# Hybrid decoder trunk: the remaining input projections are put between the attention steps

## The reference

```python
for l in range(DEPTH):                     # DEPTH = 2, SEQ = 512, D_MODEL = 1024
    h = rmsnorm(x, norm_mix_pre[l])
    z = h @ w_in[l]
    z_sc, z_cf, z_moba, z_mla = jnp.split(z, SPLITS, axis=-1)
    y_a = short_conv_mixer(z_sc, conv_a[l])                    # B * causal_dwconv3(C * h')
    y_b = conformer_conv_mixer(z_cf, conv_b[l], ...)           # GLU, depthwise conv of 31 taps, LayerNorm, swish
    y_c = moba_attention(z_moba, cos_c, sin_c)                 # 4 heads of 64
    y_d = mla_attention(z_mla, g_q, g_kv, w_uq, w_ukv, ...)    # latents 384 and 128, 4 heads of 96
    y = jnp.concatenate([y_a, y_b, y_c, y_d], axis=-1) @ w_out[l]
    x = x + rmsnorm(y, norm_mix_post[l])
    f = conv_ffn_block(rmsnorm(x, norm_ffn_pre[l]), w_ffn_up[l], conv_ffn[l], w_ffn_down[l])
    x = x + rmsnorm(f, norm_ffn_post[l])
```

## Time and profile before

| what | value |
|---|---|
| median of 3 runs | 1291.59 us |
| the runs | 1283.93, 1291.59, 1292.61 us |
| profiled execution, whole | 1292.75 us |
| its span (first to last instruction) | 1291.0 us |
| mean granted TensorE clock | 0.967 |
| PE, PEld, DVE, ACT, POOL busy | 95%, 80%, 66%, 46%, 18% |

### The profile page before, as it was taken

One profiled execution on the slowest core, in us unless ns is written; L12 is line 12 of the kernel. 1 busy time (PEld: TensorE's weight loads), 2 busy tenths in 40 slices (PEclk: granted clock), 3 DMA queues, 4 the chain that ended last, 5 costly groups with the idle time before them and its releaser, 6 DMA issues.

```text
span 1291.0 us, 15584 instructions
## 1 busy us (share of the span) xinstructions
PE 1227.7 (95%) x6036; PEld 1032.0 (80%) x6036; DVE 847.3 (66%) x1178; ACT 591.7 (46%) x889; POOL 233.3 (18%) x208
## 2 busy tenths in 40 slices
PE   5997999999999999999999799999899999999997
PEld 5885878888888888888898587788788888888885
DVE  4699576587666666544669977565686666665453
ACT  3453367454444444434545534664454444444432
POOL 1284167020000000000006733551100000000000
PEclk8998988999999999999999999599999999999998
DMA  7222202352333333456632230025333333335563
GB/s 235 78 67 82 76 1 82 115 162 84 98 98 95 94 94 97 156 190 210 196 96 78 63 92 33 1 86 173 101 114 98 98 98 96 95 96 185 181 215 128
DMA packets 155676, 143.17 MB, mean 111 GB/s; under 512 B 6447, under 2 KB 137427, under 8 KB 155603
## 3 DMA queue, kind: packets, MB, share of 16 engines
q1 hardware_dynamic: 154480, 140.40, 35.7%
q10 hardware_dynamic: 1123, 1.79, 0.4%
HBM read 140.07 MB, written 2.10 MB: 110 GB/s over the span
## 4 chain that ended last, share of the span: by engine, by line
PE 80%; DVE 12%; POOL 3%; issue 2%; DMA 2%; ACT 1%; SPq 0%; POOLq 0%; DVEq 0%; ACTq 0%
PE ps L459 26%; PE ps L460 25%; PE ps L461 25%; DVE cf_out L1040 4%; DVE wsp L391 2%; PE ps L670 2%; POOL prob L805 1%; POOL rms_r L763 1%; DMA x<-in_x 1%; DVE rot L937 1%; DVE xn L881 1%; DMA raw<-in_w_ffn_up 1%; DVE shuf L935 1%; DVE hid L942 1%; PE ps L514 1%
## 5 line engine op out<-in xcount | busy, mean ns | idle before, releaser
L459 PE MATMUL ps<-xn,wsp 128*128 128x512 f32 (+2 forms) x1136 | 421.6, 371 | 20.8 <-DVE xn L881 15.9
L460 PE MATMUL ps<-xn,wsp 128*128 128x512 f32 (+2 forms) x1136 | 418.4, 368 | 0.0
L461 PE MATMUL ps<-xn,wsp 128*128 128x512 f32 (+2 forms) x1136 | 418.2, 368 | 0.0
L391 DVE TENSOR_TENSOR wsp<-raw,wsp 128x1024 fp32r<-128x1024 f32 (+2 forms) x250 | 306.6, 1228 | 160.5 <-ACT wsp L383 160.3
L383 ACT ACTIVATE wsp<-raw 128x1024 fp32r<-128x1024 f32 (+1 forms) x256 | 266.9, 1043 | 186.3 <-PE ps L461 152.2
L459 PEld LDWEIGHTS ps<-xn,wsp 128*128 128x128 f32 (+1 forms) x1136 | 217.0, 191 | 59.1 <-DVE xn L881 18.1
L461 PEld LDWEIGHTS ps<-xn,wsp 128*128 128x128 f32 (+1 forms) x1136 | 216.6, 191 | 35.5
L460 PEld LDWEIGHTS ps<-xn,wsp 128*128 128x128 f32 (+1 forms) x1136 | 216.9, 191 | 35.0 <-issue 0.5
L459 PE MATMUL ps<-wsp,hid 128*128 128x512 f32 (+1 forms) x488 | 189.7, 389 | 0.0
L461 PE MATMUL ps<-wsp,hid 128*128 128x512 f32 (+1 forms) x488 | 189.1, 388 | 0.0
L460 PE MATMUL ps<-wsp,hid 128*128 128x512 f32 (+1 forms) x488 | 189.1, 387 | 0.0
(11 more groups left out here) (136 smaller groups left out, 1367.6 us busy)
## 6 DMA issues: line engine op xcount, KB each, us to landing
raw<-in_w_ffn_up SPq DMA_DIRECT2D x88, 512.0 KB, 3.8
raw<-in_w_ffn_down SPq DMA_DIRECT2D x88, 512.0 KB, 3.9
raw<-in_w_in SPq DMA_DIRECT2D x40, 512.0 KB, 3.8
raw<-in_w_out SPq DMA_DIRECT2D x32, 512.0 KB, 3.5
x<-in_x SPq DMA_DIRECT2D x4, 512.0 KB, 9.6
out_x<-x SPq DMA_DIRECT2D x4, 512.0 KB, 3.9
raw<-in_w_uq SPq DMA_DIRECT2D x4, 288.0 KB, 2.9
gain_mix<-in_norm_mix_post SPq DMA_DIRECT2D x2, 512.0 KB, 4.8
```

Of the source, the lines that this page charges most:

```text
L391: eng.tensor_tensor(wsp[:, u % SPLIT, 1, 0:nk * n], raw[:, (l * NU + u) % RAW, 0:nk * n], fp(wsp[:, u % SPLIT, 0, 0:nk * n]), ALU.subtract ...
L459: pe.matmul(dst, a[0], b[0], start=start, stop=False, skip_group_check=True)
L460: pe.matmul(dst, a[0], b[1], start=False, stop=False, skip_group_check=True)
L461: return pe.matmul(dst, a[1], b[0], start=False, stop=stop, skip_group_check=True)
```

## The change

Groups 10 and up lose their place ahead of attention. After group 10 (`ckv`) the attention loop begins at once, and the other projections, the MLA products, the three `stat` and `spread` pairs and the mean of the LayerNorm are issued by `fill(p)` at the head of the steps `p` that the table `AT` names. They share two PSUM banks, 4 and 7, in turn, and each waits until the one before the last has been taken out of its bank (`weave_free`). The loop has 34 places: two without scores lie between the MoBA and the MLA heads. The splits of the weights are put at the steps of `SPLIT_AT`. W_out's order of rows becomes `OUT_ORDER`, and seven rows of its first half are issued in the last eight places of the loop. Of the conformer's second half DVE does the first 7 taps, ACT and POOL the other 24 (6 ahead of the loop, 18 in it, one a step); of the first half 10 taps lie ahead of the loop and 21 in it. MLA queries, keys and values get tiles in `hid` in place of `xn`, since `xn` is still read. The scaled rows and the exponentials share one buffer of four (`sp`), where `sm` had two and `prob` three.

```diff
+OUT_ORDER = (4, 5, 0, 1, 6, 2, 3, 7)
+
+
+G_CF, G_QK, G_V, G_CKV = 0, 4, 8, 10
+GROUP = dict(ckv=10, cq0=11, cq1=12, cq2=13, sc0=14, kr=15, mq0=16, mq1=17, mk0=18, mk1=19, sc1=20, mq2=21, mq3=22,
+             mk2=23, sc2=24, mv0=25, mv1=26, mk3=27, sc3=28, sc4=29, sc5=30)
+G_UP = 31
 NG = G_UP + 2 * NF
...
+SCORE0, PT_BANKS, PV_BANKS = 5, (2, 3), (0, 1)
 RING = (0, 1, 2, 3, 5, 6, 7)
-PV_BANKS = (0, 1, 7)
+WEAVE_BANKS = (4, 7)
+WEAVE = ("ckv", "cq0", "stat_ckv", "cq1", "spread_ckv", "cq2", "stat_cq", "sc0", "spread_cq", "kr", "mq0", "mq1", "mk0",
+         "mk1", "sc1", "mq2", "mq3", "mk2", "sc2", "mv0", "mv1", "mk3", "mean", "sc3", "sc4", "stat_ln", "sc5",
+         "spread_ln")
+
+AT = dict(cq0=1, stat_ckv=2, cq1=3, spread_ckv=4, cq2=5, stat_cq=8, sc0=8, spread_cq=10, kr=11, mq0=14, mq1=14, mk0=15,
+          mk1=15, sc1=16, mq2=17, mq3=17, mk2=18, sc2=19, mv0=20, mv1=20, mk3=21, mean=23, sc3=24, sc4=26, stat_ln=27,
+          sc5=29, spread_ln=30)
 UP_BANKS = (4, 5, 6, 7)
...
-CF_VECTOR = {3: 2, 4: 1, 5: 1, 6: 1, 7: 1, 8: 4, 9: 4, 10: 4, 11: 2, 12: 4, 13: 4, 14: 3}
-CF_SCALAR = {3: 1, **{g: 3 for g in range(4, 14)}}
-assert sum(CF_VECTOR.values()) == CF_TAPS and sum(CF_SCALAR.values()) == CF_TAPS
+
+
+CF_LEAD = 7
+CF_SECOND = {3: 2, 4: 1, 5: 1, 6: 1, 7: 1, 8: 1}
+CF_FIRST = {8: 2, 9: 3, 10: 5}
+CF_SCALAR = {8: 2, 9: 2, 10: 2}
+CF_FIRST_STEP = {**{p: 1 for p in range(18)}, 2: 2, 6: 2, 10: 2}
+CF_SCALAR_STEP = {p: 1 for p in range(18)}
+assert sum(CF_SECOND.values()) == CF_LEAD
+assert sum(CF_FIRST.values()) + sum(CF_FIRST_STEP.values()) == CF_TAPS
+assert sum(CF_SCALAR.values()) + sum(CF_SCALAR_STEP.values()) == CF_TAPS - CF_LEAD
 N_ATT = 2 * HEADS * TC
-NPROB = 3
+NPROB = 4
 TRAIL = 3
-VALUES_AFTER = (3, 5, 6)
+VALUES_AFTER = (3, 5, 5)
+
+GAP = 2
+N_STEP = N_ATT + GAP
 ATT_TAIL = TRAIL + 5
+ROWS_AT = N_STEP
+
+SPLIT_AT = {2: 14, 4: 15, 6: 16, 8: 17, 10: 18, 13: 19, 15: 20, 22: 21, 23: 22, 25: 23, 26: 24, 27: 25, 29: 26, 31: 27}
+SPLIT_AT.update({ROWS_AT + 1 + j: U_OUT + 4 + j for j in range(7)})
+POOL_SPLITS = (U_OUT, U_OUT + 1, U_OUT + 2)
+
+
+def step_at(p):
+
+    if 0 <= p < N_ATT // 2:
+        return p
+    if N_ATT // 2 + GAP <= p < N_STEP:
+        return p - GAP
+    return None
+
+
+def head_at(h):
+    return h * TC + (GAP if h >= HEADS else 0)
 
 
...
+                def between(name, u, rhs, m=P, c0=0):
+
+                    weights_ready(l, u)
+                    weave_free(l, name)
+                    dense(u, weave_bank(name), rhs, m=m, c0=c0).then_inc(group_done, 1)
...
+                def fill(p):
+
+                    for ev in ("ckv", "cq", "ln"):
+                        if p == AT["stat_" + ev]:
+                            stat(ev, l)
+                        if p == AT["spread_" + ev]:
+                            spread(ev, l)
+                    for j in range(3):
+                        if p == AT[f"cq{j}"]:
+                            between(f"cq{j}", 11 + j, x_pairs)
+                    if p == AT["kr"]:
+                        between("kr", U_KR, x_pairs, m=MLA_QK)
+                    for h in range(HEADS):
+                        if p == AT[f"mq{h}"]:
+                            if h == 0:
+                                pe.wait_ge(lat_ready, l * 4 + 4)
+                            between(f"mq{h}", U_UQ[h // 2], [pair(hid[:, CQN + j]) for j in range(3)],
+                                    m=MLA_QK, c0=(h % 2) * MLA_QK)
...
+                weights_ready(l, G_CKV)
+                weave_free(l, "ckv")
+                dense(G_CKV, weave_bank("ckv"), x_pairs).then_inc(group_done, 1)
+                for p in range(N_STEP + ATT_TAIL):
+                    fill(p)
...
+                    if s is not None:
+                        transposes(s)
+                    for h in range(2 * HEADS):
+                        for part, after in enumerate(VALUES_AFTER):
+                            if p == head_at(h) + TRAIL + after:
+                                values(h, part)
+                    if ROWS_AT <= p < ROWS_AT + KD - 1:
+                        out_row(0, p - ROWS_AT)
+                for i in range(ROWS_AT + KD - 1 - ROWS_AT, KD):
+                    out_row(0, i)
+                for i in range(KD):
+                    out_row(1, i)
+                    if i in (4, 6):
...
+                conv_i = 0
+                for _ in range(sum(CF_SCALAR.values())):
+                    conv_add(conv_i)
+                    conv_i += 1
+                pool.wait_ge(rope_in, 32)
+                for p in range(N_STEP + ATT_TAIL):
+                    for _ in range(CF_SCALAR_STEP.get(p, 0)):
+                        conv_add(conv_i)
+                        conv_i += 1
+                    t = step_at(p)
+                    if t is not None:
+                        n = (t % TC + 1) * P
+                        pool.wait_ge(inv_done, l * N_ATT + t + 1)
+                        pool.tensor_tensor(sp[:, t % NPROB, 0:n], sp[:, t % NPROB, 0:n],
+                                           rowinv[:, t:t + 1].to_broadcast([P, n]), ALU.mult).then_inc(prob_done, 1)
+                    if p == 2:
+                        rsqrt("ckv", l)
+                    if p in (5, 6):
+                        add_square("cq", p - 4, l)
+                    if p == 8:
...
+                        rsqrt("cq", l)
+                    if p in (14, 15):
+                        query_sin(p - 14)
+                        query_sum(p - 14)
...
+                for p in range(N_STEP + ATT_TAIL):
+                    t, s, e = step_at(p), step_at(p - TRAIL), step_at(p - 1)
+                    if t is not None:
+                        n = (t % TC + 1) * P
                         dve.wait_ge(ident_set, 6)
                         dve.wait_ge(score_done, l * N_ATT + t + 1)
-                        if t >= 2:
-                            dve.wait_ge(exp_done, l * N_ATT + t - 1)
-                        dve.tensor_tensor_reduce(out=sm[:, t % 2, 0:n], in0=ps[:, SCORE0 + t % 2, 0:n],
+                        if t >= NPROB:
+                            dve.wait_ge(pt_done, l * N_ATT + t - NPROB + 1)
+                        dve.tensor_tensor_reduce(out=sp[:, t % NPROB, 0:n], in0=ps[:, SCORE0 + t % 2, 0:n],
                                                  in1=causal[:, T - n:T],
                                                  scale=-(MOBA_SCALE if t < N_ATT // 2 else MLA_SCALE), scalar=3e38,
                                                  op0=ALU.add, op1=ALU.min, accum_out=negmax[:, t:t + 1])\
...
+                    if p in SPLIT_AT and SPLIT_AT[p] not in POOL_SPLITS:
+                        if SPLIT_AT[p] == POOL_SPLITS[-1] + 1:
+                            dve.wait_ge(lo_done, l * NU + SPLIT_AT[p])
+                        split_lo(dve, l, SPLIT_AT[p])
+                    if p == AT["stat_ckv"]:
+                        event_var("ckv", l)
+                    if p == AT["spread_ckv"]:
+                        latent_scaled("ckv", (3,))
+                    if p == AT["spread_ckv"] + 2:
+                        latent_lo(3)
+                    if p == AT["stat_cq"]:
+                        event_var("cq", l)
+                    if p == AT["spread_cq"]:
+                        latent_scaled("cq", range(3))
+                    if p == AT["kr"]:
+                        key_rope()
+                    if p == 12:
...
+                    for _ in range(CF_FIRST_STEP.get(p, 0)):
+                        conv_tap(0, taps_taken[0])
+                        taps_taken[0] += 1
...
+                    if p in SPLIT_AT:
+                        split_hi(act, l, SPLIT_AT[p])
+                    if p == 0:
+                        latent(3, "ckv")
+                        act.wait_ge(lat_in, l * 4 + 1)
+                        square("ckv", 0, lat[:, 3, :], l)
```

855 lines of the change are left out of this document (439 added, 416 removed).

## The result

The changed kernel takes 1386.64 us (median of 4 runs, 1385.44 to 1390.68), the kernel before 1289.69 us in the same comparison: a ratio of 1.076, 95% interval 1.073 to 1.079. That is 97 us more, where the forecast had 20 and the range ended at 1336. The direction was right, the size was not.

What follows compares the result with a forecast made beforehand. PE was taken as the bound, losing time to waits and a lower clock. Per layer, 143.8 us of work plus 44 of waits and clock loss gave 187.8, 10 more than before: 1313 us in all, range 1264 to 1336.

Steps and rivals of the forecast that it cites:

- my 143.8 us: PE's work per layer from the start of `ckv` to the end of W_out's first half, at full clock; claimed unchanged.
- The lower clock: 6: Per layer, half-rate loss after the 5.3 and 9.5 us stops at `stat_ckv` and `stat_cq`: 2 and 4 us.
- 143.8 + 44: Forecast layer time from `ckv` to W_out's first half: work plus added waits and clock loss, 187.8 us against 177.7 before.
- the stretch: From the start of `ckv` to the end of W_out's first half, per layer; predicted at 183 to 193 us.
- rival of a low clock through the MoBA steps: Clock stays low from step 2 to 17, costing 12 us more a layer: 1337 us; chance 0.11.
- thin steps: The 13 steps of the MLA half with no group in them, at 0.15 us waited per step: 2 us.
- DVE against POOL: Steps 9 to 18, both engines busy and sharing SBUF ports: 1.5 us added a layer.
- interleaving fills PE: Rival: DVE and ACT work ahead during each group, PE loses only some 20 us a layer: 1265 us; chance 0.22.
- The signs that I gave beforehand: Profile checks: three PE waits, length from `ckv` to W_out's first half, DVE near 90% busy, no stop in the tail.

## Why the prediction missed

**Right.** The direction, and the mechanism as far as it went: PE waits for a chain through four engines, and the work stays (my 143.8 us left out the small things; by the windows it is 148.3 before and 147.2 after). The waits that it followed step by step are there, in us: `stat_ckv` 5.3 forecast, 4.63 measured; `spread_ckv` 2.5 and 3.14; `stat_cq` 9.5 and 9.58; `spread_cq` 2.0 and 3.46; `mq0` 4.8 and 6.06; `mk0`, `sc1` and `mk2` 9.1 and 2.96 + 4.46 + 2.56 = 9.98. Sum 33.2 against 36.9. Loads cost nothing (DMA share 0.15). The rows in the tail cover some 1.6 us a layer.

**The term that failed is "The lower clock: 6".** I charged the clock behind two stops only, at the rate of the one stop that the trace before showed (6.24 idle, 3.9 lost). It is 25 a layer: the changed kernel has twelve stops from 1.5 to 9.6 us, so the clock is low behind nearly every one, and a group of 24 matmuls that runs behind a stop takes 6.6 to 7.95 us in place of 5.6 to 5.7. Since 14.0 to 17.6 us of such loss were in the kernel before as well, and my sum of 143.8 + 44 put a whole layer together anew, the right entry was all of it. That is 19 of the 36.8 us by which the stretch came out longer (224.6 against 187.8). The rival of a low clock through the MoBA steps had the right sign and 12 us a layer; it left out the stops of the MLA half.

**The stops that the sum did not have** are the second part, 13.7 us (the waits that it did follow came out 3.7 longer): `sc3` waits 4.54 for a split that stands on ACT at step 22, behind that step's exponential; the tail waits 4.27 where I wrote that it has none; `sc2` waits 1.47; `mk3` waits 4.73 where I had 1.3. (The split's buffer was free 6 us before: `mk3`'s last matmul starts at 232.62, ACT's half of the split at 239.41, DVE's half at 240.48.) All are in the half in which I did not follow DVE and ACT, but took an average ("thin steps": 2). The 3.5 us for thin steps and for DVE against POOL did not come in full on top. With the work, which I had 3.4 too small, the sum closes: 19 + 13.7 + 3.7 - 3.5 + 3.4 = 36.3 of 36.8.

**What the waits hang on, I saw and did not use.** Against "interleaving fills PE" I wrote that DVE cannot work ahead, since each of its steps begins with scores that PE issues behind the group. That sentence is most of the case: with the order turned round, 61 of the 97 us come back. I took it as a fact of the design, when it is the place of one call. The signs that I gave beforehand mostly held: `stat_cq` 9.6 (7 to 11), `stat_ckv` 4.6 (about 5), `mq0` 6.1 (3 to 7). Three did not: the tail, the stretch, 224.6 for 183 to 193, and DVE, which I expected near 90% busy in steps 10 to 17 and which is busy 36.57 of the 59.78 us from `spread_cq` to `mk2`, 61%. A full DVE would have meant load; a DVE at 55% beside a PE at 77% over the whole stretch means turns.

The Trainium skill, "Perfetto Trace Analysis", section "Optimization Strategy", says that interleaving regimes with different busiest engines may improve performance. Here it cost 7.6% as written, and 1.5% in the best order tried. By the same section one looks for the gaps of the engine that should be full and for what would let the dependence start sooner; that is what found the line.

**Theories that fell on the way:** DVE's load (22 us of 97 with the taps left out), the place of most of the latents beside attention (nothing), the order of groups against waits alone (-19, then +11), the two banks (nothing in time). The order of a step against its group holds, with the two groups ahead of waits and POOL's order for 16 more. **Open:** the chain of `cq` with no step of attention in it, a bank that nobody else uses, and the last 20 us between 1309.5 and the kernel before. In that kernel idle time is 25.2 against 13.8 and the clock's loss 13.6 against 14.0, so 11 us a layer of stops remain; each would have to be followed on DVE and ACT, as in the tail, and that was not tried.
